# Stick-breaking attention on one core: scores, values and sums in a new step order, and the absolute value taken on ScalarE

## The chip, the cores and the metric

The kernel runs on one core of a Trainium2 chip. A core has five engines that run their own instruction streams and meet at semaphores: TensorE (PE, matrix products, with a separate row PEld for weight loads), VectorE (DVE), ScalarE (ACT), GpSimd (POOL) and SyncE (SP), which here only issues transfers. The metric is the time of one execution on the device in microseconds (us), as the median of several executions; lower is better.

## What is computed

The program is two transformer blocks over 256 tokens of width 1024. The change lies in the attention of the first block, "stick-breaking" attention with 16 heads of 64. Cut to what matters:

```python
def stick_breaking_attention(q, k, v):
    z = einsum('bhqd,bhkd->bhqk', q, k) / sqrt(64)
    mask = s_idx < t_idx
    log1m = where(mask, -softplus(z), 0.0)
    excl = cumsum(log1m, axis=3, reverse=True) - log1m
    a = where(mask, exp(log_sigmoid(z) + excl), 0.0)
    return einsum('bhqk,bhkd->bhqd', a, v)
```

Before it the first block runs a pooling mixer and an MLP (width 4096), then the projections for keys, values and queries. After it come the output projection, a second MLP, and then the second block: an input projection, a gated convolution, a differential attention, an output projection and a mixture of 32 experts, whose weights come as three pieces of 2 MB for each expert.

The kernel computes the softplus as max(z, 0) + ln(1 + exp(-|z|)).

## The kernel before

**Staging.** All weights come from HBM in chunks of 2 MB into a ring of four slots, issued by SyncE. A chunk is split into a high and a low part in quarters (`w_hi` on ScalarE at L1082, `w_lo` on VectorE at L1378), and each product runs as three matrix products (L599 to L601). A slot of the ring may be loaded again when its last quarter has been split (`lo_ready`); the expert weights wait for slots in the same manner. Nothing is loaded on behalf of the first attention: its inputs `kT`, `qT` and `v` are already in SBUF.

**The attention.** The 16 heads are worked in eight pairs (`PAIRED` is 8); m is the number of the pair. Keys lie on the 128 partitions, and the two heads of a pair have 384 columns each: 256 queries for the first block of keys and 128 for the second. A pair has these pieces:

- `scores(m)` on TensorE (L728, L731, L734: 10 matmuls): the scores z of the pair and the mask into two banks of PSUM. Three pairs of banks take turns (m % 3), so the scores of pair m wait until the exponent of pair m-3 has read them (`prob_ready`).
- max(z, 0) on VectorE (L1464), into `att[.., m%2, 1]`, called t below.
- L1465 on VectorE, z - 2 max(z, 0) = -|z|, into `att[.., m%2, 0]`, called e below; it signals `absz_ready`.
- exponent (L1162) and logarithm with bias 1 (L1163) on ScalarE, in place on e.
- t + e on VectorE (L1457), the softplus; it signals `lp_ready`.
- `args(m)` on TensorE (L743, L745: 8 matmuls): subtracts the sums of the softplus from z in PSUM, by a triangular matrix and a matrix of ones. These are "the sums".
- exponent on ScalarE from PSUM (L1170) into `att[.., m%2, 2]`; it signals `prob_ready`.
- `weighted(m)` on TensorE (L756, L759: 8 matmuls): the product with the values, into one of two banks (m % 2), which must have been emptied of pair m-2 (`oT_ready`).
- output copy on ScalarE (L1174, `mixT_hi`) and the remainder on VectorE (L1469, `mixT_lo`), which signals `oT_ready`.

Each engine runs a loop over steps i, written by hand, and takes its pieces strictly in this order:

```
PE  step i:  args(i-2), scores(i), weighted(i-3)
ACT step i:  exponent and logarithm of i, exponent from PSUM of i-2, output copy of i-4
DVE step i:  t+e of i-1, max of i, L1465 of i, remainder of i-4
```

`order(...)` makes an engine wait for the end of its own instruction. The output projection `project` (L599 to L601 on `mixT`) begins after the last `weighted`. ScalarE loads one set of function tables at the kernel's start (`preload_act_table_set`).

Of the kernel before, what the change touches and what calls it, by code (L numbers as in the profile page):

```python
# [8 lines left out]
T = 256  # L9
# [7 lines left out]
PAIRED = HEADS // 2  # L17
# [14 lines left out]
ALU = mybir.AluOpType  # L32
ACT = mybir.ActivationFunctionType
# [118 lines left out]
def build(nc, a, out):  # L152
    ctx = ExitStack()
    with ctx:
        def sem(name):
            return ctx.enter_context(nc.semaphore(name))
# [4 lines left out]
        def at(name, shape, offset, dt=F32):  # L161
            return nc.alloc_sbuf_tensor_at(name, shape, dt, offset=offset)
# [49 lines left out]
        mixT_hi = at("mixT_hi", [P, KD, T], w_base + 32 * K, F32R)  # L212
# [19 lines left out]
        att = at("att", [P, 2, 3, 2, 384], scratch)  # L232
# [9 lines left out]
        ps = ctx.enter_context(nc.psum_tensor("ps", [P, 8, COLS], F32))  # L242
        acc = ps[:, 0:4, :].rearrange("p (t b) c -> p t (b c)", t=TT)

        def wk(b):
            return ps[:, 4 + b, :]
# [61 lines left out]
        oT_hi = sem("oT_hi")  # L308
# [33 lines left out]
        z_done = sem("z_done")  # L342
        absz_ready = sem("absz_ready")
        log_ready = sem("log_ready")
        lp_ready = sem("lp_ready")
        arg_done = sem("arg_done")
        prob_ready = sem("prob_ready")
        o_done = sem("o_done")
# [244 lines left out]
        def _(pe):  # L593
# [127 lines left out]
            def zpair(m):  # L721
                return ps[:, 2 * (m % 3):2 * (m % 3) + 2, :]

            def scores(m):

                z = zpair(m)
                for r in (0, 64):
                    mm(z[:, r // 64, 0:T], kT[r:r + 64, m, 0:P], qT[r:r + 64, m, :], start=True, stop=False,  # L728
                       skip_group_check=True)
                for r in (0, 64):  # L730
                    mm(z[:, r // 64, T:T + P], kT[r:r + 64, m, P:T], qT[r:r + 64, m, P:T], start=False, stop=False,  # L731
                       skip_group_check=True)
                for c in range(2):
                    last = mm(z[:, c, 0:384].rearrange("p (b t) -> p b t", t=P)[:, 0:3:2, :], identr[:, :],  # L734
                              strictr[:, :].unsqueeze(1).to_broadcast([P, 2, P]), start=False, stop=True,
                              skip_group_check=True)
                last.then_inc(z_done, 1)

            def args(m):
                z, lp = zpair(m), att[:, m % 2, 1, :, :]  # L740
                pe.wait_ge(lp_ready, m + 1)
                for c in range(2):
                    mm(z[:, c, 0:384], ntri, lp[:, c, :], start=False, stop=False, skip_group_check=True)  # L743
                for c in range(2):
                    last = mm(z[:, c, P:T], nones, lp[:, c, T:T + P], start=False, stop=True, skip_group_check=True)  # L745
                last.then_inc(arg_done, 1)

            def weighted(m):
                p = att[:, m % 2, 2, :, :]
                o = wk(2 + m % 2)  # L750
                pe.wait_ge(prob_ready, m + 1)
                if m >= 2:

                    pe.wait_ge(oT_ready, m - 1)
                for c in range(2):
                    mm(o[64 * c:64 * c + 64, 0:T], v[:, 0, (2 * m + c) * DH:(2 * m + c + 1) * DH], p[:, c, 0:T],  # L756
                       start=True, stop=False, skip_group_check=True)
                for c in range(2):
                    last = mm(o[64 * c:64 * c + 64, P:T], v[:, 1, (2 * m + c) * DH:(2 * m + c + 1) * DH], p[:, c, T:T + P],  # L759
                              start=False, stop=True, skip_group_check=True)  # L760
                last.then_inc(o_done, 1)
# [2 lines left out]
            pe.wait_ge(maskr_ready, 2)  # L764
            pe.wait_ge(proj_taken, 16)
            pe.wait_ge(v_taken, 4)
            for i in range(PAIRED + 3):
                if 2 <= i < PAIRED + 2:
                    args(i - 2)
                if i < PAIRED:  # L770
                    if i >= 3:

                        pe.wait_ge(prob_ready, i - 2)
                    scores(i)
                if i >= 3:
                    weighted(i - 3)

            def project(m):

# [91 lines left out]
            for p in range(STEPS):  # L871
# [23 lines left out]
                else:  # L895
                    m = p - OUT
# [134 lines left out]
        def _(act):  # L1031
            order = Order(act, act_order)
            fn = nc.scalar.activation
# [121 lines left out]
                    ahead(n, f)  # L1155


            for i in range(PAIRED + 4):
                if i < PAIRED:
                    e = att[:, i % 2, 0, :, :]  # L1160
                    act.wait_ge(absz_ready, i + 1)
                    order(fn(e, e, ACT.Exp))  # L1162
                    fn(e, e, ACT.Ln, bias=1.0).then_inc(log_ready, 1)  # L1163
                if 2 <= i < PAIRED + 2:
                    m = i - 2
                    act.wait_ge(arg_done, m + 1)
                    if m >= 2:

                        act.wait_ge(o_done, m - 1)
                    fn(att[:, m % 2, 2, :, :], ps[:, 2 * (m % 3):2 * (m % 3) + 2, 0:384], ACT.Exp).then_inc(prob_ready, 1)  # L1170
                if i >= 4:
                    m = i - 4
                    act.wait_ge(o_done, m + 1)
                    fn(mixT_hi[:, m, :], wk(2 + m % 2)[:, 0:T], ACT.Copy).then_inc(oT_hi, 1)  # L1174
            for n in (N_WO, N_WO + 1):
                for f in range(4):
                    ahead(n, f)
# [137 lines left out]
        def _(dve):  # L1315
            order = Order(dve, dve_order)
            ve = nc.vector
# [132 lines left out]
                for s in range(TT):  # L1450
                    ve.tensor_copy(v[:, s, i * COLS:(i + 1) * COLS], acc[:, s, i * COLS:(i + 1) * COLS]).then_inc(v_taken, 1)

            for i in range(PAIRED + 4):
                if 1 <= i <= PAIRED:
                    t = att[:, (i - 1) % 2, 1, :, :]
                    dve.wait_ge(log_ready, i)
                    ve.tensor_tensor(t, t, att[:, (i - 1) % 2, 0, :, :], ALU.add).then_inc(lp_ready, 1)  # L1457
                if i < PAIRED:
                    z, t = ps[:, 2 * (i % 3):2 * (i % 3) + 2, 0:384], att[:, i % 2, 1, :, :]
                    dve.wait_ge(z_done, i + 1)  # L1460
                    if i >= 2:

                        dve.wait_ge(arg_done, i - 1)
                    order(ve.tensor_scalar(t, z, 0.0, None, ALU.max))  # L1464
                    ve.scalar_tensor_tensor(att[:, i % 2, 0, :, :], t, -2.0, z, ALU.mult, ALU.add).then_inc(absz_ready, 1)  # L1465
                if i >= 4:
                    m = i - 4
                    dve.wait_ge(oT_hi, m + 1)
                    ve.tensor_tensor(mixT_lo[:, m, :], wk(2 + m % 2)[:, 0:T], mixT_hi[:, m, :].bitcast(F32), ALU.subtract)\  # L1469
                      .then_inc(oT_ready, 1)  # L1470
# [282 lines left out]
```

## Time and profile before

| | before |
|---|---|
| time, median of 3 runs | 1189.21 us (1184.12, 1189.39, 1189.21) |
| time of the profiled execution | 1188.13 us |
| its span in the profile | 1186.2 us |
| its mean granted TensorE clock | 0.914 of full speed |
| stretch from the first matmul of the attention's scores to the first of the output projection | 306.23 to 357.25 us |

The profile is one execution. Its span goes from the first to the last instruction recorded; 1.9 us of the execution's time lie around it. Its clock says which part of full speed TensorE was granted on average. The attention is 51.0 us of the span, 4.3%.

### The profile page before, as it was taken

What the parts mean: (1) busy time and instruction counts of PE and PEld (TensorE: products, weight loads), DVE (VectorE), ACT (ScalarE), POOL (GpSimd) and SP (SyncE); (2) the same over time, 40 slices, a digit from 0 to 9 for tenths busy, and PEclk for the clock granted to TensorE, in tenths of its full rate; (3) what the DMA queues carried; (4) which work ended last, traced back from release to release, by engine and by line L of the source; (5) the groups of instructions that cost most, each with busy time, mean ns of one, the idle gap of its engine ahead of it and who ended that gap; (6) DMA issues with size and microseconds to landing.
All of it is one profiled execution on the core that took longest, in us unless ns stands there. A gap on an engine that the chain in (4) does not pass through costs nothing.

```text
span 1186.2 us, 14708 instructions
## 1 busy us (share of the span) xinstructions
PE 957.2 (81%) x5929; PEld 715.6 (60%) x5929; DVE 487.4 (41%) x746; ACT 374.7 (32%) x633; POOL 1.9 (0%) x7
## 2 busy tenths in 40 slices
PE   5799999699778899999698887966666676666666
PEld 4799999599546899899588764431323142424232
DVE  3655655654545656556656674220202020201010
ACT  3545544554343545445454441100000000000000
POOL 0000000000000000000000000000000000000000
PEclk9899999899999899999899998996979787878889
DMA  9454554445103445545250477699999999999996
GB/s 361 185 212 155 199 212 150 150 145 211 71 1 142 151 152 212 192 161 212 72 179 35 181 292 307 281 431 429 429 433 430 430 431 431 433 431 431 429 427 248
DMA packets 62731, 310.34 MB, mean 262 GB/s; under 512 B 2529, under 2 KB 3553, under 8 KB 52321
## 3 DMA queue, kind: packets, MB, share of 16 engines
q1 hardware_dynamic: 62256, 308.17, 64.7%
q0 software_dynamic: 432, 1.57, 0.4%
q8 instruction: 31, 0.51, 0.2%
q14 instruction: 12, 0.09, 0.0%
HBM read 308.68 MB, written 1.05 MB: 261 GB/s over the span
## 4 chain that ended last, share of the span: by engine, by line
PE 64%; DMA 16%; DVE 12%; ACT 5%; issue 2%; SPq 1%; DVEq 0%; ACTq 0%
DMA ring<-in_w_exp_down 16%; PE ps L599 14%; PE ps L600 13%; PE ps L601 13%; PE ps L976 6%; PE ps L995 5%; PE ps L957 5%; PE ps L1007 2%; DVE w_lo L1392 2%; DVE hT_lo L1365 1%; SPq L558 1%; ACT h L1039 1%; PE ps L618 1%; ACT w_hi L1097 1%; PE ps L651 1%
## 5 line engine op out<-in xcount | busy, mean ns | idle before, releaser
L1378 DVE TENSOR_TENSOR w_lo<-ring,w_hi 128x1024 fp32r<-128x1024 f32 x162 | 195.2, 1223 | 114.1 <-ACT w_hi L1082 114.1
L599 PE MATMUL ps<-hT_hi,w_hi 128*128 128x256 f32 x736 | 213.1, 290 | 9.9 <-DVE hT_lo L1365 7.9
L600 PE MATMUL ps<-hT_lo,w_hi 128*128 128x256 f32 x736 | 210.8, 286 | 0.0
L601 PE MATMUL ps<-hT_hi,w_lo 128*128 128x256 f32 x736 | 210.6, 286 | 0.0
L976 PE MATMUL ps<-ring,x 128*32 128x512 f32 x992 | 133.4, 698 | 75.2 <-DMA ring<-in_w_exp_up 65.2
L1082 ACT ACTIVATE w_hi<-ring 128x1024 fp32r<-128x1024 f32 x162 | 168.9, 1053 | 73.3 <-PE ps L601 67.5
L599 PEld LDWEIGHTS ps<-hT_hi,w_hi 128*128 128x128 f32 x736 | 143.8, 195 | 12.8 <-issue 10.8
L600 PEld LDWEIGHTS ps<-hT_lo,w_hi 128*128 128x128 f32 x736 | 143.8, 195 | 0.8 <-issue 0.2
L601 PEld LDWEIGHTS ps<-hT_hi,w_lo 128*128 128x128 f32 x736 | 143.7, 195 | 0.0
L976 PEld LDWEIGHTS ps<-ring,x 128*32 128x32 f32 x992 | 40.3, 126 | 162.8 <-issue 162.8
L995 PE MATMUL ps<-ring,moe 128*32 128x512 f32 x512 | 70.6, 712 | 53.9 <-DMA ring<-in_w_exp_down 52.6
L599 PE MATMUL ps<-w_hi,aT_hi 128*128 128x512 f32 x256 | 99.8, 390 | 0.0
L600 PE MATMUL ps<-w_lo,aT_hi 128*128 128x512 f32 x256 | 99.8, 390 | 0.0
L601 PE MATMUL ps<-w_hi,aT_lo 128*128 128x512 f32 x256 | 99.6, 389 | 0.0
L995 PEld LDWEIGHTS ps<-ring,moe 128*32 128x32 f32 x512 | 19.3, 128 | 99.5 <-issue 94.6
L957 PEld LDWEIGHTS ps<-moe,h 128*128 128x128 f32 x256 | 62.2, 334 | 5.5 <-DVE moe L1694 3.0
L957 PE MATMUL ps<-moe,h 128*128 128x128 f32 x256 | 61.6, 402 | 2.9 <-DVE moe L1694 2.9
L1133 ACT ACTIVATE rT<-ps 128x256 f32<-128x256 f32 x64 | 24.5, 383 | 120.6 <-PE ps L601 120.6
L1708 DVE COPY x<-ps 128x512 f32<-128x512 f32 x8 | 5.5, 691 | 131.9 <-PE ps L995 131.9
L1432 DVE TENSOR_TENSOR aT<-rT 128x256 f32<-128x256 f32 x64 | 27.2, 425 | 66.7 <-ACT rT L1133 66.7
L601 PEld LDWEIGHTS ps<-w_hi,aT_lo 128*128 128x128 f32 x256 | 48.0, 188 | 10.0
L599 PEld LDWEIGHTS ps<-w_hi,aT_hi 128*128 128x128 f32 x256 | 48.1, 188 | 9.6
(241 smaller groups left out, 1058.8 us busy)
## 6 DMA issues: line engine op xcount, KB each, us to landing
ring<-in_w_exp_down SPq DMA_DIRECT2D x32, 2048.0 KB, 19.5
ring<-in_w_exp_gate SPq DMA_DIRECT2D x31, 2048.0 KB, 18.9
ring<-in_w_exp_up SPq DMA_DIRECT2D x31, 2048.0 KB, 21.8
ring<-in_w_up SPq DMA_DIRECT2D x16, 2048.0 KB, 7.8
ring<-in_w_down SPq DMA_DIRECT2D x16, 2048.0 KB, 7.6
ring<-in_w_in SPq DMA_DIRECT2D x6, 2048.0 KB, 8.1
ring<-in_w_kv SPq DMA_DIRECT2D x4, 2048.0 KB, 9.4
ring<-in_w_q SPq DMA_DIRECT2D x2, 2048.0 KB, 8.1
```

The lines of the kernel that those rows point to most:

```text
L599: mm(out, a_hi, b_hi, start=start, stop=False, skip_group_check=True)
L600: mm(out, a_hi, b_lo, start=False, stop=False, skip_group_check=True)
L601: return mm(out, a_lo, b_hi, start=False, stop=stop, skip_group_check=True)
L957: last = mm(wk(2 + k // 4)[:, (k % 4) * P:(k % 4 + 1) * P], h[:, s, k:D:KD], G[:, s, :], start=(s == 0), stop=(s == TT - 1))
L976: last = mm(wk(side)[q, :], xgT[:, k, q], w4[:, j, k % 2, :] if opening else w[j][:, k, :], start=(k == 0), stop=(k == KD - 1))
L995: last = mm(wk(2 + half)[q, :], actT[:, f, q], w4[:, j, c] if by_rows else w[j][:, f, c], start=(f == 0), stop=(f == 3))
L1007: mm(acc[:, s, half * COLS:(half + 1) * COLS], S[:, s * P:(s + 1) * P], ysb[:, half * COLS:(half + 1) * COLS], start=False, stop=False, sk ...
L1082: fn(w_hi[:, f, :].rearrange("p (k w) -> p k w", k=KD), src, ACT.Copy).then_inc(hi_ready, 1)
L1133: fn(rT[:, f, :], wk(f)[:, 0:T], ACT.Relu).then_inc(relu_ready, 1)
L1378: ve.tensor_tensor(w_lo[:, f, :].rearrange("p (k w) -> p k w", k=KD), src, w_hi[:, f, :].rearrange("p (k w) -> p k w", k=KD).bitcast(F32), ...
L1392: ve.tensor_tensor(w_lo[:, p % 4, :].rearrange("p (k w) -> p k w", k=KD), quarter(n, f), w_hi[:, p % 4, :].rearrange("p (k w) -> p k w", k ...
L1432: ve.tensor_tensor(aT[:, f, :], rT[:, f, :], rT[:, f, :], ALU.mult).then_inc(sq_full, 1)
```

## The change

The three loops are reordered and the absolute value moves to another engine:

```
PE  step i:  scores(i), weighted(i-2), args(i-1)
ACT step i:  Abs of i from PSUM, output copy of i-3, exponent (scale -1) and logarithm of i, exponent from PSUM of i-1
DVE step i:  t+e of i-1, max of i, remainder of i-3
```

L1465 is gone from VectorE. ScalarE writes |z| to e with a new instruction that waits for the scores (`z_done`) and, because it overwrites e, for the sum t+e of pair i-2 (`lp_ready`). It signals `absz_ready`, for which VectorE's max now waits in place of `z_done`. The exponent takes -1 as its scale. Each of PE's, ACT's and DVE's loops has one step less.

```diff
@@ -764,16 +764,16 @@
             pe.wait_ge(maskr_ready, 2)
             pe.wait_ge(proj_taken, 16)
             pe.wait_ge(v_taken, 4)
-            for i in range(PAIRED + 3):
-                if 2 <= i < PAIRED + 2:
-                    args(i - 2)
+            for i in range(PAIRED + 2):
                 if i < PAIRED:
                     if i >= 3:
 
                         pe.wait_ge(prob_ready, i - 2)
                     scores(i)
-                if i >= 3:
-                    weighted(i - 3)
+                if i >= 2:
+                    weighted(i - 2)
+                if 1 <= i <= PAIRED:
+                    args(i - 1)
 
             def project(m):
 
@@ -1155,23 +1155,29 @@
                     ahead(n, f)
 
 
-            for i in range(PAIRED + 4):
+            for i in range(PAIRED + 3):
                 if i < PAIRED:
                     e = att[:, i % 2, 0, :, :]
+                    act.wait_ge(z_done, i + 1)
+                    if i >= 2:
+
+                        act.wait_ge(lp_ready, i - 1)
+                    fn(e, ps[:, 2 * (i % 3):2 * (i % 3) + 2, 0:384], ACT.Abs).then_inc(absz_ready, 1)
+                if i >= 3:
+                    m = i - 3
+                    act.wait_ge(o_done, m + 1)
+                    fn(mixT_hi[:, m, :], wk(2 + m % 2)[:, 0:T], ACT.Copy).then_inc(oT_hi, 1)
+                if i < PAIRED:
                     act.wait_ge(absz_ready, i + 1)
-                    order(fn(e, e, ACT.Exp))
+                    order(fn(e, e, ACT.Exp, scale=-1.0))
                     fn(e, e, ACT.Ln, bias=1.0).then_inc(log_ready, 1)
-                if 2 <= i < PAIRED + 2:
-                    m = i - 2
+                if 1 <= i <= PAIRED:
+                    m = i - 1
                     act.wait_ge(arg_done, m + 1)
                     if m >= 2:
 
                         act.wait_ge(o_done, m - 1)
                     fn(att[:, m % 2, 2, :, :], ps[:, 2 * (m % 3):2 * (m % 3) + 2, 0:384], ACT.Exp).then_inc(prob_ready, 1)
-                if i >= 4:
-                    m = i - 4
-                    act.wait_ge(o_done, m + 1)
-                    fn(mixT_hi[:, m, :], wk(2 + m % 2)[:, 0:T], ACT.Copy).then_inc(oT_hi, 1)
             for n in (N_WO, N_WO + 1):
                 for f in range(4):
                     ahead(n, f)
@@ -1450,21 +1456,20 @@
                 for s in range(TT):
                     ve.tensor_copy(v[:, s, i * COLS:(i + 1) * COLS], acc[:, s, i * COLS:(i + 1) * COLS]).then_inc(v_taken, 1)
 
-            for i in range(PAIRED + 4):
+            for i in range(PAIRED + 3):
                 if 1 <= i <= PAIRED:
                     t = att[:, (i - 1) % 2, 1, :, :]
                     dve.wait_ge(log_ready, i)
                     ve.tensor_tensor(t, t, att[:, (i - 1) % 2, 0, :, :], ALU.add).then_inc(lp_ready, 1)
                 if i < PAIRED:
                     z, t = ps[:, 2 * (i % 3):2 * (i % 3) + 2, 0:384], att[:, i % 2, 1, :, :]
-                    dve.wait_ge(z_done, i + 1)
+                    dve.wait_ge(absz_ready, i + 1)
                     if i >= 2:
 
                         dve.wait_ge(arg_done, i - 1)
                     order(ve.tensor_scalar(t, z, 0.0, None, ALU.max))
-                    ve.scalar_tensor_tensor(att[:, i % 2, 0, :, :], t, -2.0, z, ALU.mult, ALU.add).then_inc(absz_ready, 1)
-                if i >= 4:
-                    m = i - 4
+                if i >= 3:
+                    m = i - 3
                     dve.wait_ge(oT_hi, m + 1)
                     ve.tensor_tensor(mixT_lo[:, m, :], wk(2 + m % 2)[:, 0:T], mixT_hi[:, m, :].bitcast(F32), ALU.subtract)\
                       .then_inc(oT_ready, 1)
```

## Rows read from the trace of the kernel before

**Rows 1.** The page: span, and busy time of each engine

```profile
span 1186.2 us, 14708 instructions
...
PE 957.2 (81%) x5929; PEld 715.6 (60%) x5929; DVE 487.4 (41%) x746; ACT 374.7 (32%) x633; POOL 1.9 (0%) x7
```

**Rows 2.** Windows: length, busy PE, PEld, DVE, ACT, POOL, PEclk, DMA share, GB/s

```profile
306.00:357.25 51.25, 35.73 (x208) 24.08 (x208) 25.09 (x32) 21.10 (x31) 0.00 (x0) 0.93 0.00 0
780.00:900.00 120.00, 77.31 (x487) 37.19 (x488) 15.93 (x26) 6.63 (x16) 0.00 (x0) 0.83 1.01 431
```

**Rows 3.** Timeline, one step, ScalarE and VectorE: start, length, engine, line

```profile
336.83 0.84 ACT L1162 ACTIVATE att<-att 128x768 f32<-128x768 f32 x1 [3.21 <-DVE att L1465]
...
337.70 0.84 ACT L1163 ACTIVATE att<-att 128x768 f32<-128x768 f32 x1
338.45 0.79 ACT L1170 ACTIVATE att<-ps 128x768 f32<-128x768 f32 x1
339.14 0.38 ACT L1174 ACTIVATE mixT_hi<-ps 128x256 fp32r<-128x256 f32 x1
...
339.55 0.42 DVE L1469 TENSOR_TENSOR mixT_lo<-ps,mixT_hi 128x256 fp32r<-128x256 f32 x1 [2.75 <-ACT mixT_hi L1174]
...
339.89 0.95 DVE L1457 TENSOR_TENSOR att<-att 128x768 f32<-128x768 f32 x1
...
340.76 0.95 DVE L1464 TENSOR_SCALAR att<-ps 128x768 f32<-128x768 f32 x1
...
341.74 0.95 DVE L1465 SCALAR_TENSOR_TENSOR att<-att,ps 128x768 f32<-128x768 f32 x1
...
342.73 0.84 ACT L1162 ACTIVATE att<-att 128x768 f32<-128x768 f32 x1 [3.21 <-DVE att L1465]
```

**Rows 4.** Timeline, TensorE: one step, and the attention's end

```profile
345.20 0.70 PE L728 MATMUL ps<-qbuf,kbuf 64*128 64x256 f32 x4 [0.17 <-ACT att L1170]
...
346.49 0.65 PE L756 MATMUL ps<-att,vbuf 128*64 128x256 f32 x4
...
347.29 1.56 PE L743 MATMUL ps<-att,consts 128*128 128x384 f32 x4
348.68 0.61 PE L745 MATMUL ps<-att,consts 128*128 128x128 f32 x4
...
356.45 0.65 PE L756 MATMUL ps<-att,vbuf 128*64 128x256 f32 x4 [0.92 <-DVE mixT_lo L1469]
...
357.25 0.50 PE L599 MATMUL ps<-w_hi,mixT_hi 128*128 128x512 f32 x1
```

**Rows 5.** Timeline, all engines, the start of the attention

```profile
306.23 0.70 PE L728 MATMUL ps<-qbuf,kbuf 64*128 64x256 f32 x4 [1.47 <-DVE vbuf L1451]
...
307.62 0.96 DVE L1464 TENSOR_SCALAR att<-ps 128x768 f32<-128x768 f32 x1 [1.54 <-PE ps L734]
...
309.60 0.84 ACT L1162 ACTIVATE att<-att 128x768 f32<-128x768 f32 x1 [9.19 <-DVE att L1465]
...
312.37 1.86 PE L743 MATMUL ps<-att,consts 128*128 128x384 f32 x4 [3.49 <-DVE att L1457]
...
315.01 1.23 PE L728 MATMUL ps<-qbuf,kbuf 64*128 64x256 f32 x4
```

**Rows 6.** Windows of 1 us, columns as in rows 2

```profile
314.00:315.00 1.00, 1.00 (x5) 0.77 (x3) 0.17 (x1) 0.80 (x1) 0.00 (x0) 0.50 0.00 0
342.00:343.00 1.00, 1.00 (x2) 0.70 (x3) 0.70 (x1) 0.27 (x1) 0.00 (x0) 0.50 0.00 0
```

**Rows 7.** Groups by line and shape, whole kernel

```profile
L1170 ACT ACTIVATE att<-ps 128x768 f32<-128x768 f32 x8 | 6.4, 797 | 2.5 <-PE ps L745 2.5
...
L1100 ACT ACT_TABLE_LOAD x1 | 1.3, 1283 | 0.7 <-PEq L1741 0.7
```

**Rows 8.** Waits of SyncE's transfer queue, whole kernel

```profile
SPq L558 <- PE ps L976: 275.5, 19, 31.3
...
SPq L558 <- DVE w_lo L1392: 15.7, 3, 6.1
```

## The prediction

> **What bounds the kernel now.** I read the page first. Its share of busy time [rows 1] makes TensorE the likely bound of the whole, but that is an average, and the change touches one stage only. So I found the stage by the instructions that read and write `att` and asked for its window [rows 2]: in 51.25 us TensorE is busy for 35.7 us (70%), VectorE for 25.1, ScalarE for 21.1, and the transfer engines for nothing. No engine is full, so a ring of waits sets the pace. The timeline shows it. From one exponent of L1162 to the next pass 342.73 - 336.83 = 5.90 us [rows 3]. All of it can be walked through on two engines: exponent 0.87 (start to start), logarithm to exponent from PSUM 0.75, that to the output copy 0.69, copy to remainder on VectorE 0.41, to t+e 0.34, to max 0.87, to L1465 0.98, and back to the exponent 0.99; the sum is 5.90. The reader is to see that TensorE isn't in that ring. VectorE can't add t+e because it stands in order behind the remainder, that waits for the copy, and the copy stands at the end of ScalarE's step. TensorE does its step in a burst and then waits.
>
> **What TensorE needs for a step.** From the first matmul of the scores at 345.20 to the first of the values at 346.49 are 1.29 us, from there to the sums 0.80, and the sums take 348.68 + 0.61 - 347.29 = 2.00 us [rows 4]. Together 4.09 us at full clock. The 0.61 counts the last matmul to its end, which the next group can overlap by some 0.1 us, so I take 4.05, with 3.95 and 4.10 as bounds. The number of matmuls doesn't change, only their order.
>
> **What ScalarE and VectorE need for a step after.** Abs is not in the trace. Its nearest row is L1170, the same 128x768 from PSUM to `att`, at 797 ns [rows 7], or 0.69 from start to start with the copy behind it [rows 3]; from the other side the activations from SBUF take 0.84. Nothing excludes a somewhat shorter one, and 0.69 to 0.84 are my bounds; I take 0.79, and 0.69 from start to start. ScalarE's step is then Abs 0.69, copy 0.38, exponent 0.87, logarithm 0.75, exponent from PSUM 0.69: 3.38 us. VectorE's step is t+e 0.87, max 0.98, remainder 0.42: 2.3 us, as L1465 (0.95) is gone. The scale of -1 adds no instruction, and I cost it at nothing. Both steps are under TensorE's 4.05.
>
> **Do the waits between them allow 4.05?** Let step i's scores start at 0. They are done at 1.39 (306.23 to 307.62 for the first pair [rows 5]). Abs runs from 1.39 to 2.18. The copy stands between Abs and the exponent, which must wait for Abs's end anyway; it moves the exponent from 2.2 to 2.46 at most. Logarithm 3.33 to 4.17, t+e to about 5.2. The sums of that pair stand in TensorE's next step, at 4.05 + 1.29 + 0.80 = 6.14: 0.9 us to spare. The exponent from PSUM of pair i-1 can start at 4.08 (ScalarE free) and at 4.13 (its sums done at 4.09): it ends at 4.92, while the values that need it start at 4.05 + 1.29 = 5.34: 0.4 us to spare. That is the tightest place. The new waits cost nothing by the same clock. Abs waits for t+e of pair i-2, which ended before; behind it on ScalarE are the copy, the exponents and the logarithm, and its z comes at 1.39 into a step in which ScalarE was free at 0.83. VectorE's max waits for the end of Abs at 2.2, ends at 3.2, and the t+e behind it is not due before 4.2. The remainder behind max ends near 3.6, and the bank that it frees is wanted in a later step. Scores reuse banks three pairs later, their exponent was read over two steps before. So TensorE becomes the bound and all slack lies with it.
>
> **The sum.** Start: before, the first exponent began at 309.60 after max and L1465; now Abs starts at 307.62 and the exponent at 308.45, 1.15 earlier, so the first sums move from 312.37 to 311.22 [rows 5]. Pair 2's scores follow at 313.2 with TensorE at full clock, where before they began at 315.01. From there six steps of 4.05, 24.3: 337.5. In the two last steps there are no scores to cover the exponent from PSUM: 0.89 for the exponent of pair 6 and its two hand-overs, 0.80 values, 2.00 sums, 0.89, 0.80 values: 342.9. The output projection started at 357.25 [rows 4]. The stage gets 14.4 us shorter if TensorE keeps its clock; with 3.95 a step 15.0, with 4.10 14.1.
>
> **The clock.** The granted clock was 0.50, the lower level of 1.2 GHz, in two places of the stage, after the 3.5 us in which TensorE stood idle before the first sums and once in the middle [rows 5, 6]. A mean of 0.93 over 51.25 us [rows 2] is a loss of 3.6 us of full clock over both, so up to 1.8 us of time a fall where TensorE is never idle. After the change the idle stretch at the start shrinks from 3.5 to 2.3 us, and later there is almost none. I count between none and two falls: 14.4, 12.6, 10.8. I take 13.5.
>
> **Does the end move with it?** In the last 400 us the transfers run at 0.98 to 1.01 of their capacity [rows 2], and if the first expert transfer didn't depend on the attention, the gain would be lost there. But SyncE's transfers of experts wait for slots, 19 times for TensorE's L976 and three times for VectorE's splits behind the second MLP [rows 8], and nothing at all is moved during the attention [rows 2]. All of them are shifted whole. From the profiled execution, 1188.13 - 13.5 = 1174.6; the median of the runs stood 1.1 above that execution, so 1189.2 - 13.5 = **1175.7 us**.
>
> **A rule that speaks against the change.** Start from the rows: ScalarE takes 0.79 us for 128x768 from PSUM and VectorE 0.95 [rows 3]. The Trainium skill, ScalarE: Activation LUTs, Rules for kernel authors, says to give cheap elementwise functions to VectorE rather than ScalarE. By the rows it would not pay here, where ScalarE is the quicker of the two and its step has room; the sum stays as it is. The second matter is the function table. The whole trace has one table load, of 1283 ns, though copies, squares, relu, exponents and logarithms alternate [rows 7]; Abs isn't among them, so the trace can't say that it needs none.
>
> **The rivals.**
> *Table switches (slower).* If Abs isn't in the loaded set, ScalarE switches twice a step, before Abs and after. Priced by the row: 2 x 1.28 = 2.57 without and 2 x (1.28 + 0.7 idle before it) = 4.0 with a drain. ScalarE's step becomes 5.95 or 7.4 us and is the bound. The stage ends at 307.6 + 8 steps + 4.4 for the last values, sums, exponent and values: 359.6 or 371.2. Against 357.25 that is 2 to 14 us slower, 1191 to 1203, and it turns from gain to loss at 2.3 us extra a step. For it speaks only that no row shows Abs; against it, five functions shared one load. The same page of the Trainium skill (Table sets: the hidden batching unit) says that abs is in every set, and that a switch costs 2.66 us with its drain; by that price the step would be 8.7 and the time about 1213. No run here shows it yet.
> *The clock keeps falling.* In the expert stage the mean granted clock is 0.83 with TensorE busy for 64% of it [rows 2]. At 0.83 a step of 4.05 becomes 4.9; seven such steps cost 6 us: saving 8.4, time 1181. Against it: TensorE's idle time is what goes away.
> *ScalarE's ring is the bound after all.* If the hand-overs add up to over 0.4 us (Abs longer than 0.84, its read of PSUM beside TensorE's writes), the exponent from PSUM becomes late for the values, and each step takes perhaps 4.8 us: saving about 9, time 1180.
> *The gain is lost among the experts.* The transfers there are the bound and their waits may fall worse. Time 1189. The 22 waits above speak against it.
>
> **How the numbers follow.** Forecast 0.79; falling clock 0.07; ScalarE's ring 0.05; lost later 0.05; table switches 0.04. The forecast's own range: savings 10.8 to 15.0, and a run of before lay 5 us under its median, so a median may lie some us off: 1169 to 1179. The two middle rivals take the top to 1181.5, which leaves the last two outside, and I let the bottom go to 1168.5. A measurement of this kernel tells about 0.5% from no change, 6 us, so under 1183.3 is faster. Faster: 0.79 + 0.07 + 0.05, less 0.02 for runs that scatter: 0.89. Within 0.5%: 0.07. Slower: 0.04, table switches.
>
> **What would show it.** Right: scores of neighbouring pairs 4.0 to 4.1 us apart; from the first scores to the first matmul of the output projection some 36.5 to 39 us; TensorE over 90% busy in it; Abs rows of 0.8 us; one table load in the page; TensorE waiting for nothing from pair 2 on; the windows behind it as long as before. Wrong: more than one table load; steps of 4.8 or more with TensorE's sums or values waiting for ScalarE's L1170 counterpart; a granted clock of 0.5 in more than two places; or expert transfers that start no earlier than before.

## The result and the profile after

The changed kernel takes 1179.32 us in the median of 4 runs (1178.35 to 1179.95), the kernel before 1189.3 (1184.12 to 1189.53). The medians are 10.0 us apart. The ratio of the two kernels is 0.9925 with a 95% interval of 0.9903 to 0.9946, so the changed one is faster by 0.75%. The forecast was 1175.7. The profiled execution took 1179.16 us, its span is 1177.4. Two later comparisons of the same code gave 0.9919 [0.9891, 0.9947] and 0.992 [0.9897, 0.9943].

The page of the changed kernel, the lines that answer to [rows 1]:

```profile
span 1177.4 us, 14722 instructions
...
PE 958.2 (81%) x5929; PEld 717.2 (61%) x5929; DVE 481.0 (41%) x738; ACT 381.5 (32%) x641; POOL 1.9 (0%) x7
```

The stretch from the first matmul of the scores to the first of the output projection, and one stretch of the experts, with the columns of [rows 2]:

```profile
307.23:346.62 39.39, 35.16 (x208) 23.76 (x208) 18.21 (x23) 27.72 (x39) 0.00 (x0) 0.91 0.00 1
780.00:900.00 120.00, 76.84 (x500) 35.13 (x490) 15.93 (x26) 6.64 (x16) 0.00 (x0) 0.83 1.01 431
```

The attention takes 39.39 us where it took 51.02. TensorE is busy for 35.2 us of it (89%), with the work that had filled 70%. The stretch of the experts looks as before.

The timeline of ScalarE and VectorE over one step, answering to [rows 3]. L1165 is Abs, L1169 the copy, L1172 and L1173 exponent and logarithm, L1180 the exponent from PSUM, L1470 max, L1474 the remainder, L1463 t+e:

```profile
325.18 0.81 ACT L1180 ACTIVATE att<-ps 128x768 f32<-128x768 f32 x1
...
326.47 0.81 ACT L1165 ACTIVATE att<-ps 128x768 f32<-128x768 f32 x1 [0.47 <-PE ps L734]
...
327.18 0.38 ACT L1169 ACTIVATE mixT_hi<-ps 128x256 fp32r<-128x256 f32 x1
327.31 0.96 DVE L1470 TENSOR_SCALAR att<-ps 128x768 f32<-128x768 f32 x1 [1.18 <-ACT att L1165]
327.44 0.84 ACT L1172 ACTIVATE att<-att 128x768 f32<-128x768 f32 x1
...
328.30 0.42 DVE L1474 TENSOR_TENSOR mixT_lo<-ps,mixT_hi 128x256 fp32r<-128x256 f32 x1
328.32 0.84 ACT L1173 ACTIVATE att<-att 128x768 f32<-128x768 f32 x1
...
329.19 0.96 DVE L1463 TENSOR_TENSOR att<-att 128x768 f32<-128x768 f32 x1 [0.47 <-ACT att L1173]
329.20 0.81 ACT L1180 ACTIVATE att<-ps 128x768 f32<-128x768 f32 x1
...
330.49 0.81 ACT L1165 ACTIVATE att<-ps 128x768 f32<-128x768 f32 x1 [0.47 <-PE ps L734]
```

From one Abs to the next pass 4.02 us, and now Abs is what waits, for TensorE. VectorE's remainder at 328.30 no longer holds up t+e, which starts at 329.19, as soon as the logarithm of 328.32 has ended. TensorE's timeline over the same step and to the end of the stretch, answering to [rows 4]:

```profile
325.07 0.70 PE L728 MATMUL ps<-qbuf,kbuf 64*128 64x256 f32 x4
...
326.36 0.65 PE L756 MATMUL ps<-att,vbuf 128*64 128x256 f32 x4
...
327.16 1.56 PE L743 MATMUL ps<-att,consts 128*128 128x384 f32 x4
...
329.09 0.70 PE L728 MATMUL ps<-qbuf,kbuf 64*128 64x256 f32 x4
...
342.12 0.65 PE L756 MATMUL ps<-att,vbuf 128*64 128x256 f32 x4 [0.90 <-ACT att L1180]
...
342.92 1.56 PE L743 MATMUL ps<-att,consts 128*128 128x384 f32 x4
...
345.82 0.65 PE L756 MATMUL ps<-att,vbuf 128*64 128x256 f32 x4 [0.90 <-ACT att L1180]
...
346.62 0.50 PE L599 MATMUL ps<-w_hi,mixT_hi 128*128 128x512 f32 x1
```

Scores 1.29, values 0.80, sums up to the next scores 1.93: 4.02 us with nothing between. The two waits at 342.12 and 345.82 (0.90 each, for L1180) are the two last steps, which have no scores to cover them. The start, answering to [rows 5]:

```profile
307.23 0.70 PE L728 MATMUL ps<-qbuf,kbuf 64*128 64x256 f32 x4 [1.47 <-DVE vbuf L1457]
...
308.63 0.81 ACT L1165 ACTIVATE att<-ps 128x768 f32<-128x768 f32 x1 [7.21 <-PE ps L734]
...
309.47 0.84 ACT L1172 ACTIVATE att<-att 128x768 f32<-128x768 f32 x1
...
312.31 2.93 PE L743 MATMUL ps<-att,consts 128*128 128x384 f32 x4 [2.43 <-DVE att L1463]
...
318.32 0.65 PE L756 MATMUL ps<-att,vbuf 128*64 128x256 f32 x4
...
321.06 0.70 PE L728 MATMUL ps<-qbuf,kbuf 64*128 64x256 f32 x4
```

The first sums begin 5.08 us after the first scores (before 6.14). But the step that they begin takes until 321.06: from the first sums to the first values 6.01 us where at full clock it would be 1.93 + 1.29 = 3.22. The granted clock in it, answering to [rows 6]:

```profile
312.30:318.30 6.00, 5.99 (x18) 3.96 (x18) 1.78 (x2) 2.12 (x3) 0.00 (x0) 0.50 0.00 1
```

The table and the activations, answering to [rows 7], and the transfer waits, answering to [rows 8]:

```profile
L1180 ACT ACTIVATE att<-ps 128x768 f32<-128x768 f32 x8 | 6.5, 812 | 5.5 <-PE ps L745 5.3
L1165 ACT ACTIVATE att<-ps 128x768 f32<-128x768 f32 x8 | 6.5, 809 | 11.1 <-PE ps L734 11.1
...
L1100 ACT ACT_TABLE_LOAD x1 | 1.3, 1283 | 0.7 <-PEq L1746 0.7
```

```profile
SPq L558 <- PE ps L976: 275.5, 19, 31.3
```

One table load is still all there is, and the expert transfers wait 19 times for the same line for the same 275.5 us. Where the time came from and went is read from the first matmul record of each part, as the trace of each execution has it (us; the changed kernel's first trace is the one above, the other runs are described below):

| stretch | before | before, again | changed | changed, again | changed, third | one gap filled | all gaps filled |
|---|---|---|---|---|---|---|---|
| start to first scores | 306.2 | 306.9 | 307.2 | 305.9 | 307.9 | 305.8 | 303.0 |
| the attention | 51.0 | 51.9 | 39.4 | 36.6 | 39.4 | 36.6 | 36.6 |
| output projection and second MLP | 225.1 | 225.1 | 226.2 | 225.6 | 226.2 | 225.6 | 222.9 |
| second block up to the first expert | 156.6 | 156.2 | 157.4 | 153.4 | 157.4 | 156.7 | 152.4 |
| first expert to the end | 447.3 | 447.3 | 447.2 | 447.4 | 446.9 | 446.7 | 446.9 |

In the first pair of traces the attention gave 11.6 us; the parts around it took 1.0, 1.1 and 0.8 back, and the experts' part moved as a whole. That leaves two questions: is the step really set by TensorE, with every part of the change needed for it, and what took back 2.8 us inside the attention's first step (6.01 against 3.22) and 2.9 outside?

### The profile page after: what moved, and what is told of

Its sections match the earlier page's. It is cut to its first block, busy times and chain, and to the rows that moved or that the text cites. A ratio compares the mean times of both kernels' runs of the same rounds, so it can differ in the third digit from the quotient of the medians.

```text
span 1177.4 us, 14722 instructions
## 1 busy us (share of the span) xinstructions
PE 958.2 (81%) x5929; PEld 717.2 (61%) x5929; DVE 481.0 (41%) x738; ACT 381.5 (32%) x641; POOL 1.9 (0%) x7
## 4 chain that ended last, share of the span: by engine, by line
PE 67%; DMA 16%; DVE 9%; ACT 4%; issue 2%; SPq 1%; DVEq 0%
DMA ring<-in_w_exp_down 16%; PE ps L599 14%; PE ps L600 14%; PE ps L601 14%; PE ps L976 6%; PE ps L995 6%; PE ps L957 5%; PE ps L1007 2%; DVE w_lo L1398 1%; PE ps L743 1%; SPq L558 1%; ACT h L1039 1%; PE ps L618 1%; DVE hT_lo L1371 1%; ACT w_hi L1097 1%
## 5 line engine op out<-in xcount | busy, mean ns | idle before, releaser
L599 PEld LDWEIGHTS ps<-hT_hi,w_hi 128*128 128x128 f32 x736 | 146.2, 199 | 12.5 <-issue 11.0
```

The lines of the kernel that those rows point to most:

```text
L599: mm(out, a_hi, b_hi, start=start, stop=False, skip_group_check=True)
```

## The experiments

### Which part of the change does it

**Abs only.** All orders and lags as before, only the absolute value on ScalarE.

```diff
+                    act.wait_ge(z_done, i + 1)
+                    if i >= 2:
+                        act.wait_ge(lp_ready, i - 1)
+                    fn(e, ps[:, 2 * (i % 3):2 * (i % 3) + 2, 0:384], ACT.Abs).then_inc(absz_ready, 1)
                     act.wait_ge(absz_ready, i + 1)
-                    order(fn(e, e, ACT.Exp))
+                    order(fn(e, e, ACT.Exp, scale=-1.0))
...
-                    dve.wait_ge(z_done, i + 1)
+                    dve.wait_ge(absz_ready, i + 1)
...
-                    ve.scalar_tensor_tensor(att[:, i % 2, 0, :, :], t, -2.0, z, ALU.mult, ALU.add).then_inc(absz_ready, 1)
```

> Only the absolute value moves to ScalarE; all three loops keep the orders and lags of before. Theory (TensorE's 4.0 us a step is the bound only if both parts of the change are made; here a ring of ScalarE and VectorE waits remains, because the remainder on VectorE still waits for the copy at the end of ScalarE's step): about 4.7 us a step, the stretch from the first scores to the output projection about 42 to 44 us against 51.0 before and 39.4 after. Rival (the gain comes wholly from the work taken off VectorE, the order does nothing): 4.0 us a step and 39.4 us. Other rival (the order does it all): no gain, 51 us.

Steps took 4.70 us and the stretch 41.45, just under the range expected. The ring can be walked in the timeline (L1175 is the exponent from PSUM here):

```profile
329.01 0.81 ACT L1165 ACTIVATE att<-ps 128x768 f32<-128x768 f32 x1 [1.17 <-PE ps L734]
...
329.85 0.84 ACT L1167 ACTIVATE att<-att 128x768 f32<-128x768 f32 x1
...
330.73 0.84 ACT L1168 ACTIVATE att<-att 128x768 f32<-128x768 f32 x1
...
331.48 0.79 ACT L1175 ACTIVATE att<-ps 128x768 f32<-128x768 f32 x1
...
332.32 0.30 PEld L728 LDWEIGHTS ps<-qbuf,kbuf 64*128 64x128 f32 x4 [0.80 <-ACT att L1175]
...
333.71 0.81 ACT L1165 ACTIVATE att<-ps 128x768 f32<-128x768 f32 x1 [1.17 <-PE ps L734]
```

Abs 0.84, exponent 0.88, logarithm 0.75, exponent from PSUM to the scores that reuse its banks 0.84, scores to Abs 1.39: 4.70. Both rivals are out. The ring is not the one that I had named (the copy and the remainder). It is closed by the banks of PSUM. In the old order ScalarE's step i does the exponent from PSUM of i-2, and TensorE's next step waits for it with the scores that reuse its banks. The median was 1177.93 us (0.9919 [0.9895, 0.9943]), no longer than the changed kernel's 1179.32. So in the medians the new order adds nothing to Abs. The trace of this run had no fall of the clock in the stretch; a trace of the changed kernel without a fall (below) has 36.59 us there, 4.9 less. Most executions of the changed kernel pay 2.8 of the 4.9 us back in a fall of the clock (below), and the rest goes outside the attention, where the traces of one and the same kernel scatter by as much.

**Order only.** The new orders and lags, with L1465 back on VectorE and no Abs.

```diff
-                    act.wait_ge(z_done, i + 1)
-                    if i >= 2:
-                        act.wait_ge(lp_ready, i - 1)
-                    fn(e, ps[:, 2 * (i % 3):2 * (i % 3) + 2, 0:384], ACT.Abs).then_inc(absz_ready, 1)
...
-                    order(fn(e, e, ACT.Exp, scale=-1.0))
+                    order(fn(e, e, ACT.Exp))
...
-                    dve.wait_ge(absz_ready, i + 1)
+                    dve.wait_ge(z_done, i + 1)
...
                     order(ve.tensor_scalar(t, z, 0.0, None, ALU.max))
+                    ve.scalar_tensor_tensor(att[:, i % 2, 0, :, :], t, -2.0, z, ALU.mult, ALU.add).then_inc(absz_ready, 1)
```

> Only the orders and lags change, z - 2 max(z,0) stays on VectorE and there is no Abs. Theory: VectorE's chain max, L1465, exponent, logarithm, t+e remains a ring with VectorE's order: about 4.6 us a step, stretch 42.5 to 44 us. Rival (the absolute value on ScalarE does it all): 51 us. Rival (the order does it all): 39.4 us.

Steps of 4.60 us, stretch 43.77 with a slow first step, like the changed kernel's 39.39; median 1179.74 us (0.9933 [0.9911, 0.9954]). Here the ring is the one expected, max, L1466 (before: L1465), exponent, logarithm, t+e, and max again:

```profile
327.67 0.95 DVE L1465 TENSOR_SCALAR att<-ps 128x768 f32<-128x768 f32 x1
...
328.66 0.95 DVE L1466 SCALAR_TENSOR_TENSOR att<-att,ps 128x768 f32<-128x768 f32 x1
...
329.65 0.84 ACT L1167 ACTIVATE att<-att 128x768 f32<-128x768 f32 x1 [1.91 <-DVE att L1466]
...
330.52 0.84 ACT L1168 ACTIVATE att<-att 128x768 f32<-128x768 f32 x1
...
331.40 0.96 DVE L1458 TENSOR_TENSOR att<-att 128x768 f32<-128x768 f32 x1 [1.45 <-ACT att L1168]
...
332.27 0.95 DVE L1465 TENSOR_SCALAR att<-ps 128x768 f32<-128x768 f32 x1
```

0.99 + 0.99 + 0.87 + 0.88 + 0.87 = 4.60. So each part alone takes a step from 5.90 to 4.6 or 4.7, and only both reach TensorE's 4.02.

**Copy at the end.** The changed kernel with the copy of pair i-3 behind the exponent from PSUM.

```diff
-                if i >= 3:
-                    m = i - 3
-                    act.wait_ge(o_done, m + 1)
-                    fn(mixT_hi[:, m, :], wk(2 + m % 2)[:, 0:T], ACT.Copy).then_inc(oT_hi, 1)
...
                     fn(att[:, m % 2, 2, :, :], ps[:, 2 * (m % 3):2 * (m % 3) + 2, 0:384], ACT.Exp).then_inc(prob_ready, 1)
+                if i >= 3:
+                    m = i - 3
+                    act.wait_ge(o_done, m + 1)
+                    fn(mixT_hi[:, m, :], wk(2 + m % 2)[:, 0:T], ACT.Copy).then_inc(oT_hi, 1)
```

> The changed kernel with the output copy moved to the end of ScalarE's step, behind the exponent from PSUM, pair i-3 as before. Theory: the copy then ends late, VectorE's remainder waits for it and the sum t+e stands behind the remainder, so t+e closes a ring again: about 4.5 us a step, stretch 42 to 43 us, 3 us more than the changed kernel. Rival (the place of the copy costs nothing since TensorE is the bound): 4.02 us a step and 39.4 us.

Steps of 4.60 to 4.66 us once the copies have begun, stretch 43.47 with the same slow first step as the changed kernel's 39.39; median 1182.46 us (0.9952 [0.9938, 0.9966]). The place of the copy is worth 4.1 us, somewhat more than the 3 expected. The mechanism was again not quite the one expected. Who waits for whom over some four steps (waiter, what it waited for: us in total, times, longest):

```profile
DVE mixT_lo L1474 <- ACT mixT_hi L1180: 9.4, 4, 2.4
...
PE ps L756 <- DVE mixT_lo L1474: 1.5, 3, 0.5
```

TensorE's values wait for the remainder, which frees their bank of PSUM, and the remainder waits 2.4 us for the late copy, with t+e behind it.

### Is TensorE the bound, and how much room has ScalarE

**Abs twice.** One more activation in each step of ScalarE.

```diff
+                    fn(h[:, 0, 0:768].rearrange("p (b t) -> p b t", b=2), ps[:, 2 * (i % 3):2 * (i % 3) + 2, 0:384], ACT.Abs)
                     fn(e, ps[:, 2 * (i % 3):2 * (i % 3) + 2, 0:384], ACT.Abs).then_inc(absz_ready, 1)
```

> The changed kernel with one more Abs of 128x768 from PSUM in each step of ScalarE, into a buffer not in use: 0.7 us more of ScalarE's time a step, 5.6 us over eight steps. Theory (TensorE is the bound and ScalarE has 0.4 us to spare at its tightest place): steps of 4.1 to 4.4 us, stretch 41 to 42.5 us, so less than half of the added work is paid. Rival (ScalarE's chain is the bound already): every added 0.7 us is paid, steps of 4.7, stretch 45 us.

Steps of 4.12 and 4.15 us, stretch 40.81 (with a slow first step): 1.4 of the 5.6 us added were paid, 0.1 in each step between and the rest at the start and in the two last steps, where TensorE waits anyway. There is one execution, of 1175.42 us.

**Values twice.** The eight matmuls of each pair issued twice, 0.65 us.

```diff
-                for c in range(2):
-                    mm(o[64 * c:64 * c + 64, 0:T], ...
...
+                for _ in range(2):
+                    for c in range(2):
+                        mm(o[64 * c:64 * c + 64, 0:T], ...
...
```

> The changed kernel with the products with the values issued twice into the same bank, the same result: 0.8 us more of TensorE's time a step. Theory (TensorE is the bound): all of it is paid, steps of 4.8 us, stretch about 45.6 us. Rival (TensorE has slack, hand-overs set the 4.02 us): steps under 4.4 us, stretch under 42.5 us.

All steps 4.67 us: 0.65 more, which is all that a second set takes. The window of the stretch:

```profile
306.30:348.10 41.80, 37.57 (x273) 26.09 (x273) 18.21 (x23) 27.73 (x39) 0.00 (x0) 1.00 0.00 1
```

It took 41.80 us at full clock against 36.59 for the changed kernel at full clock (below): 5.2 us, 8 x 0.65. I had priced the set at 0.80, its whole distance to the sums, so the number was missed and the point stands: what is added to TensorE is paid in full, what is added to ScalarE by a quarter. There is one execution, of 1177.88 us.

### Where the rest went

**The same kernels again.** Both kernels were run and traced again, unchanged.

> The changed kernel unchanged, for a second trace. Theory (outside the attention the 2.8 us given back are falls of the granted clock whose place differs from execution to execution): the attention again 39.4 us or 36.7 if the clock falls elsewhere, and some of the other stages differ from the first trace of the changed kernel by about 1 us each. Rival (the change itself lengthens the later stages): the stages of the first trace to 0.2 us.

> The kernel before unchanged, for a second trace. Theory: stages outside the attention vary by about 1 us each, so that a part of the 2.8 us is scatter of the clock. Rival: the stages repeat to 0.2 us and the 2.8 us are the change's.

Seven executions of the changed kernel took 1170.75, 1170.83 and five times 1179.15 to 1180.37 us. The traced one was one of the quick ones: 1170.83. The window of its attention:

```profile
305.91:342.50 36.59, 32.37 (x209) 22.05 (x209) 18.22 (x23) 27.73 (x39) 0.00 (x0) 1.00 0.00 1
```

The clock holds at 1.00 throughout and the attention takes 36.59 us, with the code of the first trace. So the first step's 2.8 us (39.39 - 36.59) are the clock's. The columns of the table show the same outside: the second block up to the first expert took 157.4 in two traces of the changed kernel and 153.4 in this one, 156.6 and 156.2 in those of the kernel before, which repeats more closely outside the attention (by 0.7 us and less). A stretch of it, the differential attention, from the first trace of before and the second of the changed kernel:

```profile
604.51:738.94 134.43, 113.26 (x659) 92.14 (x657) 86.27 (x196) 56.60 (x118) 0.00 (x0) 0.94 0.53 204
```

```profile
590.32:721.49 131.17, 109.31 (x658) 88.14 (x656) 86.22 (x196) 56.51 (x118) 0.00 (x0) 0.98 0.54 209
```

The same work, 134.4 and 131.2 us, at 0.94 and 0.98 of the clock. For the 1.1 us of the second MLP the first 8 us of its matmuls tell, in the first trace of before and the first of the changed kernel:

```profile
391.33:399.33 8.00, 8.00 (x54) 8.00 (x55) 4.16 (x10) 4.32 (x10) 0.00 (x0) 0.79 0.01 2
```

```profile
380.70:388.70 8.00, 8.00 (x45) 8.00 (x46) 3.56 (x9) 3.89 (x8) 0.00 (x0) 0.63 0.01 2
```

TensorE is busy throughout, at a mean clock of 0.79 and 0.63. From its first matmul to the end the MLP took 191.0 us in both traces of before, 192.1 and 192.2 in the first and third of the changed kernel, and 191.5 (at 0.71) in the second. What remained after these was whether the clock's falls come from idle gaps and can be kept away.

**One gap filled.** TensorE multiplies zeros in the gap before the first sums, into a bank of PSUM that the next scores overwrite.

```diff
+                if i == 1:
+                    for _ in range(10):
+                        mm(ps[:, 4, :], zero_t[:, 0:P], zero_t[:, :], start=True, stop=True)
                 if 1 <= i <= PAIRED:
                     args(i - 1)
```

> The changed kernel with ten matmuls of zeros (128x512) into a bank not in use, between the scores of pair 1 and the first sums, so that TensorE is not idle there. They compute nothing that is used. Theory (the first step's 2.7 us over the estimate are the granted clock of 0.5 that follows TensorE's idle time): the clock stays at 1.00 in the stretch, first sums 2.0 us instead of 3.7, stretch about 36.7 us, the whole 2.7 us shorter unless later stages take it back. Rival (the slow first step is due to something else, or the zeros do not hold the clock): first sums as slow as before and the stretch 39.4 us or more.

The stretch was 36.59 us and the median 1175.46 (1173.56 to 1175.64, 4 runs), ratio to before 0.9893 [0.9873, 0.9912]. It was then run again next to the changed kernel on one chip:

> The changed kernel with ten matmuls of zeros in the first gap of the attention, again, beside the changed kernel on one chip. Theory (they prevent the fall of the clock at the start of the attention in every execution): median 3 to 4.5 us under the changed kernel's, about 1175.5, and stretch 36.6 us. Rival (the first run had a lucky clock): median within 1 us of the changed kernel's.

> The changed kernel, third trace, as the one to compare the fills with. Theory: most executions at 1178 to 1180.5 us with a fall of the clock at the start of the attention, a few near 1171 without. Rival (chips differ): all on one level.

```profile
305.81:342.40 36.59, 34.66 (x218) 23.79 (x219) 18.21 (x23) 27.74 (x39) 0.00 (x0) 1.00 0.00 1
```

With the gap filled 1174.72 us (1169.86 to 1176.04, 6 runs) and 36.59 us in the attention; without 1179.09 (1177.14 to 1180.86, 6 runs) and 39.44. Over all, 15 of 17 executions of the changed kernel lie between 1177.1 and 1180.9 us, and 10 of 10 with zeros at or below 1176.04. Of the six traces that have this gap of 2.4 us without zeros (three of the changed kernel, Abs only, copy at the end, values twice) three have the fall and three do not; the two with a longer gap there (3.1 us with Abs twice, 3.5 with order only) have it; of the four with zeros in it, two of them below, none has it. The medians are 4.4 apart, of which 2.85 are seen in the attention.

**Two gaps filled.** Six more such matmuls before the attention, where TensorE waits for the copies of the values.

```diff
             pe.wait_ge(proj_taken, 16)
+            for _ in range(6):
+                mm(ps[:, 4, :], zero_t[:, 0:P], zero_t[:, :], start=True, stop=True)
             pe.wait_ge(v_taken, 4)
```

> As head_fill, with six more matmuls of zeros before the attention while TensorE waits for the copies of the values. Theory: the clock already holds with the ten, so nothing more is gained in the attention: stretch 36.6 us, median within 1 us of head_fill2's; the six take no time since TensorE idles there for 1.5 us. Rival (the idle time before the attention counts too): another fall goes away and the median is over 1 us lower.

Stretch 36.59, median 1175.57 (1173.95 to 1176.89, 4 runs): nothing more to gain there.

**All gaps filled.** Zeros also before and behind the transposes ahead of both MLPs, and before those ahead of the key projection and of the second block's input projection; `busy` is the loop above.

```diff
+            def busy(n, b):
+                for _ in range(n):
+                    mm(ps[:, b, :], zero_t[:, 0:P], zero_t[:, :], start=True, stop=True)
...
+                busy(16 if layer == 0 else 5, 4)
                 transposes(x, x_ready, x_count)
+                busy(12, 0)
                 pe.wait_ge(hT_lo_ready, 4 * turn + 4)
...
+            busy(40, 4)
             transposes(h, h_ready, 4)
...
+            busy(12, 4)
             pe.wait_ge(mg_ready, 4)
             pe.wait_ge(ss_ready, 12)
             mlp(1, 2, 6)
...
+            busy(40, 4)
             transposes(h, h_ready, 6)
```

> As head_fill, with matmuls of zeros also in the gaps ahead of both MLPs, the key projection and the input projection of the second block, 9 us and less each, where the norms are computed. Theory (what the first trace of the changed kernel gave back outside the attention, 2.8 us, are falls of the clock after such gaps): the stretches from the first MLP matmul and from the projections behind it are each at their shortest (190.9, 70.4, 190.9, 17.9 us) or 1 us below, median 2 to 5 us under head_fill2's. Rival (the zeros stand in the way of waiting work, or the falls have other causes): no gain, or some us slower.

The median is 1165.83 us (1163.5 to 1168.26, 5 runs), ratio to before 0.9814 [0.9788, 0.984]: 13.3 us under the changed kernel on the same chip and 8.9 under the one gap filled, more than the 2 to 5 expected. The second MLP took 188.8 us from its first matmul, 2.1 less than the shortest seen so far. Windows over the gap and the start of the second MLP and over the whole time up to the experts, first of the third trace of the changed kernel, then of this one:

```profile
373.00:390.00 17.00, 12.44 (x66) 11.82 (x66) 10.02 (x21) 8.28 (x18) 0.53 (x1) 0.60 0.10 32
0.00:730.00 730.00, 654.92 (x4024) 578.22 (x4024) 415.77 (x633) 353.84 (x575) 1.92 (x7) 0.95 0.48 176
```

```profile
365.00:382.00 17.00, 15.67 (x110) 14.03 (x109) 12.16 (x25) 10.16 (x22) 0.53 (x1) 1.00 0.17 51
0.00:714.00 714.00, 668.93 (x4171) 587.34 (x4171) 415.54 (x634) 353.64 (x575) 1.92 (x7) 1.00 0.49 180
```

The clock stands at 1.00 where it stood at 0.60, and over everything ahead of the experts at 1.00 in place of 0.95. The transposes gained too: from their start to the first matmul behind them 4.33 us became 3.31 and 6.83 became 6.12, which I had not counted. The experts' part is unmoved at 446.9 us; from 780 to 1150 us its transfers run at 1.00 of their capacity.

## Why the prediction was right, and where it was off

The mechanism came as forecast, with 1179.32 us where 1175.7 had been worked out. That is 0.3 us above the 1179 that the forecast's own range allowed; it lies in the whole range because the rivals had stretched the top to 1181.5.

**The ring and the step: right.** TensorE's step came out at 4.02 us (4.05 was taken), the attention at full clock at 36.6 us (36.7 in the sum: 342.9 - 306.2). Adding work to TensorE is paid in full.

**ScalarE's step and the waits: right.** Abs took 0.81 us (0.79 to start with), and the exponent from PSUM ended at 326.0 for values that started at 326.36, 0.4 us to spare as worked out. With a second Abs, 0.69 less that room would make 0.3 us a step; 0.1 was measured, so the room is somewhat larger than worked out. TensorE was busy for 88 to 89% of the stretch, not over 90: the gap at the start and the two at the end are more of a shorter stretch than I had in mind. The stretch was to be 36.5 to 39 us; with the fall of the clock it was 39.4. The rival of ScalarE's ring falls with the steps of 4.02 us.

**What the copy costs: right by the runs.** The exponent starts 0.97 us after Abs with the copy between them (326.47 to 327.44) and 0.84 without (308.63 to 309.47), inside the room; at the end of the step it would have cost 4.1 us.

**The end moves with the attention: right.** From the first expert to the end 447.3 and 447.2 us. The windows between the attention and the experts were not as long as before, though: 1.9 us longer in the first pair of traces. Behind a shift that is whole, the rival of a gain lost among the experts falls, and so does the one of table switches: one load of 1283 ns. The Trainium skill (ScalarE: Activation LUTs, Table sets: the hidden batching unit) has abs in every set; the trace agrees.

**The clock: mis-sized.** This is the term that put 13.5 us where some 10 were measured. It said that a fall costs at most 1.8 us, and took half a fall as likely, since the gap at the start shrinks from 3.5 to 2.3 us. The gap was 2.43 us, and in two traces of three of the changed kernel the clock was at 0.50, the level of 1.2 GHz, from before the first sums to the first values: 6.0 us of TensorE's work in place of 3.2, a cost of 2.8. The 1.8 had been taken from the falls of before, which lasted 3.1 and 3.3 us (313.5 to 316.6 and 340.9 to 344.2); the one of the changed kernel lasted 6.8 us (311.5 to 318.3). Nor was the price of a fall seen in the stage before. Its falls met a TensorE that waited anyway: the one in the middle [rows 6] lay in a step of 5.90 us (339.30 to 345.20) like the one before it, and in the second trace the stage lost twice as much clock and was only 0.8 us longer:

```profile
306.87:358.73 51.86, 38.06 (x208) 25.12 (x208) 25.10 (x31) 21.11 (x31) 0.00 (x0) 0.87 0.00 0
```

With TensorE the bound each fall is paid. But the rival of a clock that keeps falling did not come: behind 318.5 us it stood at 1.00 to the end of the stretch.

The second part of the miss lay outside the stage. The sum held every other part as constant, while the first pair of traces differed there by 2.9 us. Of this 1.0 lies ahead of the attention, where the two kernels do the same, and 1.1 in the second MLP are the clock's by the windows above; for the 0.8 of the second block it is likely and not shown. Whether it is a cost of the change is open. No instruction of the change runs there, but both traces of the changed kernel at 1179 us have the longer MLP, and neither of the kernel before has. The attention at full clock took 36.6 us where it took 51.0, 14.4 less, as the sum had it for no fall. The quickest executions, 1170.8 against 1184 to 1185, are also some 14 us apart, but no such execution of the kernel before was traced, and the changed kernel's owes 4.0 us to its second block, so that this match may be chance.

The Trainium skill (TensorE: Matmul & The Clock Gate, HAM oscillation — how this bites in real kernels) says that waits between bursts of matmuls bring the clock back down, so that each burst begins slow. The trace agrees: after a gap of 2.43 us the burst ran at 0.50 in two traces of three, and with the gap filled at 1.00. In the third the burst ran at 1.00 behind the same gap.

What stays open: 1.5 of the 4.4 us between the medians with one gap filled and none. The two traces differ by 2.1 us already ahead of the attention, where nothing was filled. Open is also why most executions of the changed kernel have the fall and a few have not, with the same code; the traces show only that the falls lie at other places relative to the work. In the first trace of the changed kernel the clock fell 1.6 us into the gap, in that of before 1.1 us after the gap's end.

## What to carry to other kernels

When a stage has no full engine, walk its ring of waits start to start until the pieces add up to the step; a piece that only stands in order in front of another (here the copy and the remainder) costs as much as work. Two rings may lie just under the one that is seen: the parts of this change brought 1.2 to 1.3 us a step each and both together 1.9, where TensorE is met. Once TensorE is the bound, look at the granted clock after each of its gaps, since a fall that was hidden before is now paid (here a fall took 2.8 of the 4.9 us that the new order had won over Abs alone), and compare stage by stage over several traces before explaining two or three us.

## What the runs showed of the hardware that was not expected

TensorE's granted clock held through its gap in every trace in which it multiplied zeros there: with ten matmuls of 128x512 in a gap of 2.4 us the attention took 36.6 us in four traces of four, without them 39.4, 39.4 and 36.6. Zeros in that gap and five more places of the code took the kernel from 1179.09 to 1165.83 us, 1.1%, with no other change. Abs from PSUM took 0.81 us for 128x768 like the exponent of the same shape (0.81), and the kernel still has one table load.
